# A decoder step on one core: the samples' value product dealt over four engines instead of two

## What is computed

```python
def cross_attention(x, k, v, g, wq, wo):
    B, S, _ = x.shape
    h = rms_norm(x, g)
    q = (h @ wq).reshape(B, S, XA_HEADS, XA_HEAD_DIM)
    s = jnp.einsum('bshd,bmhd->bhsm', q.astype(jnp.float32), k.astype(jnp.float32)) * (XA_HEAD_DIM ** -0.5)
    p = jax.nn.softmax(s, axis=-1)
    o = jnp.einsum('bhsm,bmhd->bshd', p, v.astype(jnp.float32)).reshape(B, S, D_MODEL)
    return o.astype(x.dtype) @ wo
...
        xs = xs + cross_attention(xs, cache_mem_k[l], cache_mem_v[l], norm_xattn[l], xa_wq[l], xa_wo[l])
```

## Time and profile before

| what | us |
|---|---|
| median of three runs | 1138.18 |
| lowest and highest of them | 1137.84, 1140.97 |
| the profiled execution, as timed | 1140.06 |
| the profiled execution's span | 1138.3 |
| PE busy in the span | 1077.6 (95%) |
| DVE busy | 815.3 (72%) |
| ACT busy | 630.9 (55%) |
| POOL busy | 231.7 (20%) |
| the product `oS` on PE, first to last matmul | 322.94 to 342.1 |

### The profile page before, as it was taken

How to read it: one execution, slowest core, us unless ns; L and a number is a source line. 1 busy time by engine, 2 the same in 40 slices (tenths; PEclk the granted TensorE clock), 3 DMA queues, 4 the chain that set the end, 5 groups by cost and what they waited for, 6 DMA issues and landing times.

```text
span 1138.3 us, 18382 instructions
## 1 busy us (share of the span) xinstructions
PE 1077.6 (95%) x5851; PEld 793.5 (70%) x5851; DVE 815.3 (72%) x1616; ACT 630.9 (55%) x932; POOL 231.7 (20%) x197
## 2 busy tenths in 40 slices
PE   6999999899799999999999999999999999999991
PEld 5998459899449977666666666666666666666660
DVE  4734724454862355579999999999999888999993
ACT  4384333233633351566666666666667665667663
POOL 1002220001000020232222233322223332323331
PEclk7999999999999999999999999999999999999996
DMA  9502415250826181899999999999999999999945
GB/s 304 208 1 81 150 77 223 83 219 16 340 104 233 64 346 48 231 320 361 354 368 366 370 364 369 365 357 359 367 371 363 364 358 362 365 365 357 349 133 168
DMA packets 63558, 301.70 MB, mean 265 GB/s; under 512 B 13175, under 2 KB 15843, under 8 KB 36886
## 3 DMA queue, kind: packets, MB, share of 16 engines
q1 hardware_dynamic: 47038, 261.93, 60.0%
q0 software_dynamic: 16480, 39.24, 14.5%
HBM read 282.65 MB, written 36.17 MB: 280 GB/s over the span
## 4 chain that ended last, share of the span: by engine, by line
PE 86%; DMA 6%; DVE 4%; ACT 2%; issue 1%; SPq 1%; DVEq 0%; POOLq 0%; ACTq 0%
PE pair L179 17%; PE pair L1950 15%; PE pair L1975 15%; PE pair L1941 10%; PE pair L1957 7%; PE pair L1717 5%; PE pair L1928 5%; PE pair L1621 3%; DMA regB<-in_exp_w_down 2%; PE pair L1833 2%; PE pair L1901 1%; DVE regL L1154 1%; DMA regB<-in_cache_mem_k 1%; PE pair L1964 1%; DMA regA<-in_w_in 1%; PE pS L1913 1%
## 5 line engine op out<-in xcount | busy, mean ns | idle before, releaser
L758 POOL DMA_INDIRECT acc_rows<-regL x64 | 123.3, 1926 | 423.0 <-DMA acc_rows<-regL 245.5
L1975 PE MATMUL pair<-hi_parts,act_parts 128*96 128x512 f32 x512 | 163.2, 400 | 1.2 <-DVE act_parts L1559 1.2
L179 PE MATMUL pair<-h_hi,w_parts 128*128 128x260 f32 x640 | 132.2, 288 | 3.7 <-DVE h_lo L1148 3.4
L1950 PE MATMUL pair<-hi_parts,x_parts 128*96 128x512 f32 x512 | 132.4, 401 | 0.0
L179 PEld LDWEIGHTS pair<-h_hi,w_parts 128*128 128x128 f32 x640 | 105.1, 192 | 4.8 <-issue 2.8
L1975 PEld LDWEIGHTS pair<-hi_parts,act_parts 128*96 128x96 f32 x512 | 79.6, 165 | 28.2 <-DVE act_parts L1559 1.3
L1950 PEld LDWEIGHTS pair<-hi_parts,x_parts 128*96 128x96 f32 x512 | 79.8, 165 | 27.8 <-issue 1.9
L742 POOL DMA_INDIRECT regL<-h_rows,regL x67 | 68.7, 1025 | 58.7 <-DVE regL L1405 28.9
L1555 DVE TENSOR_TENSOR regB_lo<-regB,hi_parts 128x2048 fp32r<-128x2048 f32 x32 | 73.1, 2284 | 10.4 <-ACT hi_parts L1062 10.4
L1555 DVE TENSOR_TENSOR regA_lo<-regA,hi_parts 128x2048 fp32r<-128x2048 f32 x32 | 73.1, 2285 | 9.3 <-ACT hi_parts L1062 9.1
L1565 DVE TENSOR_SCALAR regL<-pair,regL 96x512 f32<-96x512 f32 x64 | 47.7, 746 | 40.7 <-PE pair L1975 40.7
(11 more groups left out here) (357 smaller groups left out, 2350.0 us busy)
## 6 DMA issues: line engine op xcount, KB each, us to landing
regA<-in_exp_w_gate SPq DMA_DIRECT2D x32, 1024.0 KB, 9.5
regA<-in_exp_w_up SPq DMA_DIRECT2D x32, 1024.0 KB, 17.0
regA<-in_exp_w_down SPq DMA_DIRECT2D x32, 1024.0 KB
regB<-in_exp_w_down SPq DMA_DIRECT2D x32, 1024.0 KB, 19.3
regB<-in_exp_w_gate SPq DMA_DIRECT2D x16, 1024.0 KB, 9.4
regB<-in_exp_w_up SPq DMA_DIRECT2D x16, 1024.0 KB, 18.3
regC<-in_exp_w_gate SPq DMA_DIRECT2D x16, 1024.0 KB, 9.0
regC<-in_exp_w_up SPq DMA_DIRECT2D x16, 1024.0 KB, 19.7
```

The costliest lines, as they stand in the source:

```text
L179: ins = pe.matmul(pair[p][:, h, 0:HALF], w, x[:, k, cols], start=k == 0 and i == 0, stop=k == KD - 1 and i == 2)
L758: pool.indirect_dma_start(acc_rows, bass.IndirectOffsetOnAxis(ap=sidx[0:SLOTS, r:r + 1].bitcast(U32), axis=0), yX[r][0:SLOTS, :], None, bo ...
L1950: pe.matmul(gu_out, x_parts[:, x, k, :], hi, start=False, stop=False, skip_group_check=True)
L1975: ins = pe.matmul(pair[2][0:SLOTS, h, :], act_parts[:, x, k, :], w[:, k, h * 512:(h + 1) * 512], start=k == 0 and s == 0, stop=k == KF - 1 ...
```

## The change

DVE keeps two tiles (6 and 7), PE keeps four (0 to 3), and tiles 4 and 5 go a new way: ACT multiplies each of their four blocks by its weights, in place, one instruction for a head (16 in all); POOL adds the four scaled blocks up into the first block of tile 4 (3 additions of 128 x 1024); and DVE adds POOL's sum to its own, head by head (4 additions of 128 x 256). Only then does PE get the sum of a head. The two new semaphores are `v_scaled` (ACT to POOL) and `p_summed` (POOL to itself and to DVE).

```diff
-BY_VECTOR = (6, 7, 4)
-BY_TENSOR = (5, 0, 1, 2, 3)
+BY_VECTOR = (6, 7)
+BY_POOL = (4, 5)
+BY_TENSOR = (0, 1, 2, 3)
...
@@ gpsimd, ahead of the wait for ss_done
+            sums_at = vc[BY_POOL[0]][:, 0, :]
+            for n in range(1, len(BY_POOL) * MT):
+                i, mt = BY_POOL[n // MT], n % MT
+                pool.wait_ge(v_scaled, n + 1)
+                if n > 1:
+                    pool.wait_ge(p_summed, n - 1)
+                pool.tensor_tensor(sums_at, sums_at, vc[i][:, mt, :], ALU.add).then_inc(p_summed, 1)
...
@@ scalar, ahead of the casts to o_hi
             J.wait_taken(a, ("o", HEADS - 1, 1))
+            a.wait_ge(pad_made, 1)
+            a.wait_ge(v_in[0], 32)
+            for i in BY_POOL:
+                for mt in range(MT):
+                    for h in range(HEADS):
+                        hs = slice(h * HD, (h + 1) * HD)
+                        ins = a.activation(vc[i][:, mt, hs], vc[i][:, mt, hs], ACT.Copy, scale=sS[:, 2 * i + mt, h:h + 1])
+                    ins.then_inc(v_scaled, 1)
             for k in range(KD):
                 a.copy(o_hi[:, k, 0:SEQ], oT[:, k, 0:SEQ]).then_inc(o_hi_made, 1)
...
@@ vector
             v.wait_ge(v_in[2], 32)
-            v.wait_ge(v_in[0], 32)
...
                     ins.then_inc(v_summed, 1)
+            n = len(BY_VECTOR) * MT
+            v.wait_ge(v_summed, HEADS * n)
+            v.wait_ge(p_summed, len(BY_POOL) * MT - 1)
+            for h in range(HEADS):
+                hs = slice(h * HD, (h + 1) * HD)
+                v.tensor_tensor(sums_at[:, hs], sums_at[:, hs], vc[BY_POOL[0]][:, 0, hs], ALU.add).then_inc(v_summed, 1)
...
@@ tensor, the product oS
-            pe.wait_ge(v_in[0], 32)
...
-                pe.wait_ge(v_summed, HEADS * (len(BY_VECTOR) * MT - 1) + h + 1)
+                pe.wait_ge(v_summed, HEADS * len(BY_VECTOR) * MT + h + 1)
```

More of the change, by code:

```diff
@@ L455, in trunk @@
         sd_landed = [sem(f"sd_landed{t}") for t in range(TT)]
+        p_summed, v_scaled = sem("p_summed"), sem("v_scaled")
         x_stored, h3_made, sg_silu, gath_zero = (sem(n) for n in ("x_stored", "h3_made", "sg_silu", "gath_zero"))
```

## The result

| | before | after |
|---|---|---|
| median of six runs, us | 1138.38 | 1145.26 |
| lowest and highest, us | 1137.84, 1140.97 | 1143.80, 1149.45 |
| profiled execution as timed, its span, us | 1140.06, 1138.3 | 1146.23, 1144.1 |
| first matmul of `oS` to first of the projection `x2`, us | 322.94 to 344.75: 21.81 | 324.43 to 352.81: 28.38 |

The ratio is 1.0057, 95% interval 1.0041 to 1.0073: slower by 6.9 us (4.7 to 8.3), by more than the 0.3% that can be told from no change. The predicted 1145.5 us with its range 1142.0 to 1148.0 held.

The account below looks back on a forecast made before the run. PE was taken to bound the kernel: it would idle 8.9 us in the first head of `oS`, ending the product 5.4 us later, plus 1.9 for half clock: 1138.18 + 7.3 = 1145.5 us, range 1142.0 to 1148.0.

Parts of the forecast that it names:

- growth of `oS`: The samples' product on PE: later end by 5.4 us at full clock, plus 1.9 for half clock, together +7.3 us.
- PE's wait in the kernel before: Inside `oS` before the change: PE waits only once, 0.33 us, for DVE's sum of the first head.
- rival "faster": POOL's relay is in time for the wait in the first head; 1134.4 if nothing waited at all; chance 0.03.
- The estimate of 2.25: One POOL addition by the Trainium skill's figures: 2.25 us, which makes the sum below 0.5 us less.
- The upper bound, 2.64: One POOL addition of 128x1024, from the slowest addition of 520 columns: 2.64 us, adding 0.6 to the forecast.
- The clock: PE after its pause in `oS`: half clock for 3.2 to 4.5 us, costing 1.6 to 2.25, taken as +1.9.
- the rival in which it doesn't come back: In `oS` after the pause: all 56 records run at half rate, +17.5 us, 1155.7; chance 0.06.
- The rival in which the clock costs little: Clock stays full in the first head, or half clock after `oS` does not come: +5.4 to +5.7, 1143.7; chance 0.12.
- What was costed at nothing: DVE's low parts and ACT's casts, covered by the later end of `oS`; the pause and half clock after it unchanged.
- first rival: The clock costs less than forecast; one case: half clock following `oS` does not come after the later `oS`, 1.6 less; chance 0.12.
- The sum on the median: Whole kernel: the runs' median of 1138.18 plus 7.3 gives 1145.5 us.
- Lost later: Behind the projection: some wait ending at a fixed time swallows the delay, 1138 to 1140; chance 0.03.

Follow-up runs that it names:

- e4: The changed kernel with 17 matmuls into an unused part of PSUM ahead of the first head's wait, so PE works through most of its pause; 1142.49 us.
- e6: The changed kernel with POOL's three additions cut to 512 of the 1024 columns; 1143.57 us, ratio to the kernel before 1.0051.
- e1: The changed kernel, but PE does the matmuls of all four heads first and takes the four sums at the end; 1137.10 us.
- e5: The changed kernel with only tile 4 on ACT and POOL (one POOL addition) and tile 5 back on PE; 1141.51 us.
- g2: Against the kernel before: DVE sums four tiles, PE four, nothing on ACT and POOL, the wait still inside each head; 1140.11 us.
- e2: As e1, with DVE making the low parts of the prompt's output ahead of its four additions of POOL's sum; 1138.96 us.
- g1: As e2, with one start flag for each PSUM bank and POOL's three additions cut to 8 of 1024 columns; 1136.32 us.

## Why the prediction was right

The mechanism was the one predicted, and each step is there. Counted from the start of `oS`:

| step | predicted | measured |
|---|---|---|
| first scaling starts | 0.78 | 0.77 |
| one scaling to the next | 0.41 | 0.40, (6.49 - 0.49) / 15 |
| first addition of POOL starts | 4.26 | 4.15 |
| one addition of 128x1024 | 2.43 | 2.34 |
| last addition ends | 11.8 | 11.5 |
| PE's pause | 8.9 | 8.43 |
| PE goes on | 12.4 | 12.05 |
| half clock behind the pause | 1.9 | 1.44 (e4) |
| growth of `oS` | 7.3 | 6.6 |

**PE's wait in the kernel before.** The prediction has PE wait 0.33 us inside `oS`. That row is the weight load's; the timeline of PE shows no idle time there, and the heads of the kernel before start 4.75 us apart from the first on (322.94, 327.69, 332.44). Only the rival "faster" counted on it, with 0.3.

**The relay's terms.** The additions are these (instructions of the line in the kernel after, ns min/median/max):

```profile
L714 POOL TENSOR_TENSOR regL<-regL x3: 2341/2343/2346, 328.6 to 333.6; 128x1024 f32<-128x1024 f32 x3
```

Scaling from 520 columns gave 2.43, 0.09 too much; e6 has 1.26 for 512. Three of them and the first one's start make up the 0.3 by which PE went on sooner. The estimate of 2.25 that the prediction worked out from the Trainium skill ("GPSIMD Engine Reference", section on elementwise accounting) was as far off on the other side. The upper bound, 2.64, was scaled from an addition that ran beside DVE and was held up by it (last section); it is not POOL's own pace.

**The clock** was put 0.5 too dear: 1.44 us lost is 2.9 us of work at half rate, where I took 3.2 to 4.5 from the earlier trace rows. Why it was shorter isn't shown. (The clock had been down for some time when PE went on, 0.70 over 331 to 335.) That it fell, and that the narrow matmuls brought it back, was right; the rival in which it doesn't come back falls with the 1.00 from 341 on. The rival in which the clock costs little is not what happened; e4, in which it costs nothing, shows what it would have given, 1142.5.

**What was costed at nothing** stayed so. DVE's low parts and ACT's casts were covered by the longer `oS`. e1 takes this cover away and shows the 2.60 that stood behind it. The pause after `oS` is unchanged, 2.65 us from its end to the projection both times (342.1 to 344.75, 350.16 to 352.81), and so is the half clock behind it: 0.54 over the projection's first 3.45 us, as before. That this can't be taken for granted is seen in e5, where it is missing and gives back 1.55; the prediction had it as "1.6 less" under its first rival.

**The rival "faster"** had its point in POOL's pace, with the wait inside the first head. e6 and g2 confirm that the wait has to be met: with half the columns, or with no relay at all, the sum is still 5.57 and 4.11 us late. What I didn't put down as the remedy is that the place of the wait, not the pace, is the cheap thing to change (e1).

**The sum on the median.** 1138.18 + 7.3 was 1145.5; measured 1145.26. Part of that agreement is luck, since the terms were 0.7 too high together, the medians grew 0.3 more than the stretch, which is within their interval, and the median of before, with six runs, lies 0.2 above that of the three runs. "Lost later" is not seen in the medians. In the profiled execution the projection starts 8.06 later than before and the span is only 5.8 longer; 2.3 us of it go again behind it. They go in the expert loop: the last matmul of line L1901 (L1923 in the kernel after) starts at 489.3 and at 497.6, still 8.3 apart, and from there to the end it is 649.0 and 646.5. The code behind that place is the same in all twelve kernels, and their traces have between 644.4 and 649.0 there. So the kernel before was profiled in an execution with the slowest loop of the twelve; what makes the loop differ isn't shown. Its executions lie 1134.8 to 1142.1 in one series.

## What to carry to other kernels

Before work is taken from the engine that bounds a stretch, look for the first instruction of that engine that needs the result: with in-order engines the whole chain that makes it has to fit ahead of that place, and a wait in the first of four heads gives it a quarter of the room that one behind all four gives. Move the wait as far back as the data allow, and only then count what the removed work is worth; the same four-tile deal on PE took 5 us off or about nothing by that alone. Add up a relay of engines link by link, with what stands behind each wait on each of them, and try the engine that finishes in time alone (here DVE, four tiles in 6.8 us more than two) before a chain of three.

## What was not expected of the hardware

**DVE and POOL held each other up.** In e2 a subtraction of two SBUF tiles on DVE took 1.74 and 2.85 us instead of 0.68 while additions of 2.35 us ran on POOL, and one of these took 2.64; each of the two subtractions ended 0.55 after the other engine's instruction. The Trainium skill ("SBUF — State Buffer", section on SBUF's two separate sides) says that VectorE and GpSimd take a shared pair of ports for a whole instruction, and that VectorE's operations with two SBUF inputs need it against GpSimd operations that read SBUF. The trace of e2 agrees, and in g1 the effect is gone with the long additions. I had expected e2 to gain 2 us on e1, but the trace of the kernel before shows the two side by side already, in the mixing sub-layer (timeline, DVE and then POOL, and DVE's instructions by line):

```profile
108.84 1.55 DVE L1239 SCALAR_TENSOR_TENSOR hT<-hT,regL 128x520 f32<-128x520 f32 x1
...
108.79 1.04 POOL L678 TENSOR_TENSOR hT<-hT 128x512 f32<-128x512 f32 x1
109.91 1.40 POOL L678 TENSOR_TENSOR hT<-regL 128x526 f32<-128x526 f32 x1
...
L1236 DVE TENSOR_TENSOR hT<-hT,regL x4: 166/850/931, 107.8 to 119.3; 128x8 f32<-128x8 f32 x4
L1239 DVE SCALAR_TENSOR_TENSOR hT<-hT,regL x4: 700/1555/1567, 108.8 to 119.6; 128x520 f32<-128x520 f32 x4
```

The last instruction of each of the two lines, at 119.3 and 119.6, stands behind POOL's last addition and takes 0.17 and 0.70; the other three of each, beside additions, take 0.82 to 0.93 and 1.55 to 1.57. The one at 108.84 ends 0.56 after POOL's addition, as in e2, and POOL's next addition takes 1.40 where the two ahead of it took 1.06 and 1.04. So that e2 risked this could have been read from rows of before.

**A short pause was enough for the half clock, and not always.** In e5 PE stood 2.60 us; the clock was still 1.00 when it went on, and fell to 0.50 (1.2 GHz) only after about 1 us of work (1.00 over 331.25 to 332.2, 0.50 over 332.6 to 335.4). The 2.65 us behind `oS`, with eight small matmuls in them, brought 0.54 in the kernels before and after and left the clock at 1.00 in e5. In the pause at 453 in the kernel before, which left it at 1.00 too, PE has no matmul for 2.25 us, since the first matmuls of that stretch end at 453.15. From these runs the length of the pause alone doesn't tell whether the clock falls.
